# Cached pages laid over 64 partitions with two keys in each, nine projection slots to a sample, and the next stage's weights loaded ahead

## The chip, the cores and the metric

One Trainium2 chip, one core. The metric is the device time of one launch in microseconds, on the slowest (here the only) core. Smaller is better.

## The reference, cut to what matters

The kernel computes one step of a two-layer decoder for a prompt of 2048 tokens and for 8 sampled sequences of one new token each. The change lies in the second layer. Its input projection gives 21 groups of 128 channels over 2056 columns (2048 prompt tokens, 8 samples) and, in a stage of its own, the values. For each of the 8 samples, stick-breaking attention runs over 4096 cached keys, which lie in 32 pages of 128 keys in an order that a page table gives:

```python
proj = jnp.einsum('btd,dn->btn', x, w_in)
k_past = cache_k[i][page_table].reshape(bs, n_pages * PAGE_SIZE, H_C, HD_C)
z = jnp.einsum('bqhd,bkhd->bhqk', qblk, kf) + bf
log_1mb = jnp.where(causal, jax.nn.log_sigmoid(-z), 0.0)
suffix = lax.cumsum(log_1mb, axis=3, reverse=True)
excl = jnp.concatenate([suffix[..., 1:], jnp.zeros_like(suffix[..., :1])], axis=-1)
att = jnp.where(causal, jnp.exp(jax.nn.log_sigmoid(z) + excl), 0.0)
out = jnp.einsum('bhqk,bkhd->bqhd', att, vf)
```

So a key's weight needs the sum of a softplus over all later keys of its sample. A key or value row of all heads is 512 floats, 2 KB; a page is 256 KB; a sample's keys and values are 16.8 MB, those of all eight 134 MB.

## The kernel before, in words

The program is a row of stages with a barrier between them. The change touches three: `project_odd` (tiles named `po_`, line 2448), `project_values` (`pv_`, line 2998) and the start of the prompt's attention (`sp_`).

**Projection in slots.** `Channels` (line 1242) multiplies x, split into a high and a low fp32r part, with weights split the same way, three matmuls for a product (`product`, lines 119 to 121). A slot is one channel group over one block of 412 columns: 8 slices of 128 rows by 3 matmuls, 24 in all. There are 105 slots in the order of `ODD_GROUPS` (line 2441). The first five run slice by slice while x comes in (`first`); each later one writes one of five PSUM banks, which ACT copies out (`evict`, line 1371) and stores (line 1303). One raw weight buffer `po_w` holds 512 KB; its split parts are doubled. At the start DVE makes the high part of each of the 8 slices of x (`split_x`), and the low parts are made by DVE (five slices) and POOL (three, `low_x`). POOL also splits all weights but the first, and ACT issues their loads.

**Sampled attention beside it.** Pages come in through `load_pages` (line 2493): for each page a register is loaded from the table, then one DMA copies 128 rows of 2 KB to the 128 partitions. Keys go through the SP queue into 3 buffers of a pair of pages, values through the ACT queue into 3 buffers of a group of 4 pages. DVE multiplies a pair of key pages by the query (line 2648) and reduces it (line 2651); after 16 pairs it adds the bias (line 2657). ACT (exponent, logarithm, exponent: lines 2612, 2616, 2621), DVE (clamp, maximum, arguments: lines 2662 to 2675) and PE (`later`, lines 2556 and 2557: sums over later keys inside a page by a triangular matrix, and of whole pages by ones) make the weights, and PE multiplies them with the values (line 2549), 8 groups of 4 pages to a sample. A key buffer is loaded again once DVE has used it, a value buffer once PE has.

What stands where in each engine's program comes from two numbers: sample b's scores are placed at slots `START + PER*b` and after, its chain at `START + PER*(b+1)`, and its value groups from four slots later on, 8 groups over `PER` slots:

```python
START, PER = 16, 10
for g in range(NS * GROUPS):
    groups.setdefault(START + PER + 4 + g * PER // GROUPS, []).append(g)
TAIL = START + PER * (NS + 1) + 6
```

The queries come from the last block of groups 0 to 3; they are transposed at slot `Q_AT`, go out to memory and come back broadcast before DVE can begin. Each engine runs its list in order, so a wait of PE for a value buffer holds up the slots behind it.

**Value projection.** `project_values` starts behind the barrier: x tile 0, eight weight slices of 512 KB, x tile 1. ACT makes the high parts of the weights, POOL and DVE the low parts of every second slice. PE's first tile goes slice by slice behind them.

Of the kernel before, what the change touches and what calls it, by code (L numbers as in the profile page):

```python
# [17 lines left out]
F32R = mybir.dt.float32r  # L18
ALU = mybir.AluOpType
# [29 lines left out]
AT_GC = AT_SP - 36096  # L49
AT_OO = AT_GC - 3 * 4 * KT * D  # L50
# [1191 lines left out]
class Channels:  # L1242
# [7 lines left out]
    def __init__(self, s, xT, w, out, groups, banks, pinned=False):  # L1250
# [8 lines left out]
        self.x_in = [s.sem(f"x_in{k}") for k in range(KT)]  # L1259
        self.x_high = [s.sem(f"x_high{k}") for k in range(KT)]  # L1260
# [32 lines left out]

    def load_x(self, sp, slices=range(KT)):
        for k in slices:
            if k >= 4:
                sp.wait_ge(self.x_ready[k - 4], 1)
            sp.dma_start(self.stage[k % 4], self.xT[:, k, :]).then_inc(self.x_in[k], 16)
# [21 lines left out]
    def split_x(self, dve, k):  # L1320
        dve.wait_ge(self.x_in[k], 16)
        high_part(dve, self.xh[:, k, :], self.stage[k % 4]).then_inc(self.x_high[k], 1)
        if k % 3 != 1:
            dve.wait_ge(self.x_high[k], 1)
            low_part(dve, self.xl[:, k, :], self.stage[k % 4], self.xh[:, k, :]).then_inc(self.x_ready[k], 1)

    def high_x(self, act, k):
        act.wait_ge(self.x_in[k], 16)
        act.copy(self.xh[:, k, :].bitcast(F32R), self.stage[k % 4]).then_inc(self.x_high[k], 1)

    def low_x_part(self, dve, k):
        dve.wait_ge(self.x_high[k], 1)
        low_part(dve, self.xl[:, k, :], self.stage[k % 4], self.xh[:, k, :]).then_inc(self.x_ready[k], 1)

    def low_x(self, pool):
        for k in range(1, KT, 3):
            pool.wait_ge(self.x_high[k], 1)
            low_part(pool, self.xl[:, k, :], self.stage[k % 4], self.xh[:, k, :]).then_inc(self.x_ready[k], 1)
# [6 lines left out]
    def first(self, pe):  # L1345
        pe.wait_ge(self.w_low, 1)
        for k in range(KT):
            pe.wait_ge(self.x_ready[k], 1)
            for t in range(self.banks):
                mm = self.part(pe, t, k)  # L1350
                if k == KT - 1:
                    mm.then_inc(self.done, 1)
# [689 lines left out]
def rwkv_chunks(nc, ops, wc, const, y, s_out, space, tail):  # L2042
# [7 lines left out]
    with Stage(nc, "rc") as s_:  # L2050
# [372 lines left out]
        def _(pool):  # L2423
# [10 lines left out]
            for t in range(STEPS):  # L2434
# [6 lines left out]
ODD_GROUPS = ([(0, range(NBLK)), (1, range(NBLK)), (2, [NBLK - 1]), (3, [NBLK - 1, *range(NBLK - 1)]),  # L2441
               (2, range(NBLK - 1))] + [(n, range(NBLK)) for n in range(4, 21)])
# [5 lines left out]
def project_odd(nc, xT, w, z, cache_k, cache_v, table, bias, const, q_rows, cat):  # L2448
# [6 lines left out]
    HR = HC * PAGES  # L2455
    with Stage(nc, "po") as s:
# [6 lines left out]
        zs = [s.sb(f"scores{q}", [P, HC, PAGES]) for q in (0, 1)]  # L2463
        e, sp_, att, mask = (s.sb(n, [P, HC, PAGES]) for n in ("e", "softplus", "att", "mask"))
        om = s.sb("om", [P, CW])
        bt, own, idt = s.sb("bias", [P, HC]), s.sb("own", [P, HC]), s.sb("id", [P, P])
        tri, one = s.sb("tri", [P, P]), s.sb("ones", [P, P])
# [11 lines left out]
        flat = lambda t: t[:, :, :].rearrange("p h r -> p (h r)")  # L2479
        START, PER = 16, 10  # L2480
        PAGES_AT = 3
# [8 lines left out]
        TAIL = START + PER * (NS + 1) + 6  # L2490
        at = lambda table, t: table.get(t, ())

        def load_pages(eng, pages, cache, b, r, sem):
            for j in range(pages.shape[1]):
                page = eng.value_load(pt[0:1, b * PAGES + PAGES - 1 - r - j:b * PAGES + PAGES - r - j], min_val=0,
                                      max_val=cache.shape[0] - 1)
                eng.dma_start(pages[:, j, :], cache[ds(page, 1)].rearrange("o k c -> k (o c)")).then_inc(sem, 16)

        @block.sync
        def _(sp):  # L2500
# [3 lines left out]
            for dst, src in ((idt[:, :], const["ident"]), (tri[:, :], const["tri"]), (own[:, :], const["own32"]),  # L2504
                             (bt[:, :], bias.broadcast_to([P, HC]))):
                sp.dma_start(dst, src).then_inc(cst, 16)
            sp.wait_ge(tab, 16)
            for k in range(KT):
                sp.wait_ge(pj.x_ready[k], 1)
# [1186 lines left out]
```

## Time and profile before

| | |
|---|---|
| median of 3 runs | 3168.12 us (3167.9 to 3170.14) |
| the profiled execution's own time | 3175.06 us |
| its span | 3173.3 us |
| busy in the span: PE | 2920.1 us, 92% |
| DVE / ACT / POOL | 2096.5 / 1276.4 / 763.2 us |
| mean rate of the DMA engines over the span | 158 GB/s |
| `project_odd` | 1504 to 2129 us |
| `project_values` | 2129 to 2355 us |

Times in the rows are microseconds from the span's start. A busy PE is not a PE at its peak, since matmuls are pipelined: one of 128 by 412 is shown with 0.35 us, while they start 0.19 us apart. The DMA share is the mean busy share of the core's 16 DMA engines; it may stand a little over 1 in a short window.

### The profile page before, as it was taken

What the parts mean: (1) busy time and instruction counts of PE and PEld (TensorE: products, weight loads), DVE (VectorE), ACT (ScalarE), POOL (GpSimd) and SP (SyncE); (2) the same over time, 40 slices, a digit from 0 to 9 for tenths busy, and PEclk for the clock granted to TensorE, in tenths of its full rate; (3) what the DMA queues carried; (4) which work ended last, traced back from release to release, by engine and by line L of the source; (5) the groups of instructions that cost most, each with busy time, mean ns of one, the idle gap of its engine ahead of it and who ended that gap; (6) DMA issues with size and microseconds to landing.
All of it is one profiled execution on the core that took longest, in us unless ns stands there. A gap on an engine that the chain in (4) does not pass through costs nothing. (4 is left out here: it accounts for less than half of the span.)

```text
span 3173.3 us, 70051 instructions
## 1 busy us (share of the span) xinstructions
PE 2920.1 (92%) x27683; PEld 2371.2 (75%) x27683; DVE 2096.5 (66%) x3274; ACT 1276.4 (40%) x2284; POOL 763.2 (24%) x711
## 2 busy tenths in 40 slices
PE   8999999978998988998899999969989999998898
PEld 7899999966776766776798887857756666667676
DVE  9526666647676647885377777614639888886576
ACT  1325555434344335352011111111228888875332
POOL 5000000012232211110311111103127666664111
PEclk9999999989999989999999999989989999999999
DMA  6624445464444556563679999865450101008342
GB/s 212 206 96 150 153 150 150 141 167 114 100 116 92 124 154 191 158 173 92 228 219 322 354 338 336 309 197 171 140 188 3 68 22 47 15 25 249 127 157 77
DMA packets 470046, 502.30 MB, mean 158 GB/s; under 512 B 200033, under 2 KB 362834, under 8 KB 464570
## 3 DMA queue, kind: packets, MB, share of 16 engines
q1 hardware_dynamic: 373034, 338.78, 35.3%
q10 hardware_dynamic: 88176, 143.03, 13.0%
q0 software_dynamic: 8512, 16.02, 1.7%
q8 instruction: 221, 3.62, 0.5%
q14 instruction: 103, 0.84, 0.1%
HBM read 356.61 MB, written 141.31 MB: 157 GB/s over the span
## 5 line engine op out<-in xcount | busy, mean ns | idle before, releaser
L2978 POOL TENSOR_TENSOR sp_att<-sp_beta,sp_left 128x512 f32<-128x512 f32 (+3 forms) x320 | 302.3, 954 | 185.9 <-DVE sp_left L2939 171.4
L119 PE MATMUL po_acc<-po_x_high,po_w_low 128*128 128x412 f32 (+1 forms) x840 | 303.8, 362 | 20.3 <-DVE po_x_low L112 14.4
L119 PE MATMUL pe_acc<-pe_x_high,pe_w_low 128*128 128x412 f32 (+1 forms) x840 | 302.5, 360 | 3.4 <-PEq L85 3.4
L120 PE MATMUL po_acc<-po_x_low,po_w_high 128*128 128x412 f32 (+1 forms) x840 | 296.6, 353 | 0.0
L121 PE MATMUL po_acc<-po_x_high,po_w_high 128*128 128x412 f32 (+1 forms) x840 | 296.6, 353 | 0.0
L120 PE MATMUL pe_acc<-pe_x_low,pe_w_high 128*128 128x412 f32 (+1 forms) x840 | 293.5, 349 | 0.0
L121 PE MATMUL pe_acc<-pe_x_high,pe_w_high 128*128 128x412 f32 (+1 forms) x840 | 293.2, 349 | 0.0
L2939 DVE TENSOR_TENSOR_SCAN sp_left<-sp_z,sp_left,sp_zero 128x512 f32<-128x512 f32 x192 | 235.7, 1269 | 18.3 <-ACT sp_z L2900 14.0
L2648 DVE TENSOR_TENSOR po_work<-po_work,po_q 128x1024 f32<-128x1024 f32 x128 | 176.2, 1377 | 66.5 <-DMA po_work<-in_cache_k 60.7
L2892 ACT ACTIVATE sp_beta<-sp_z,sp_bias 128x512 f32<-128x512 f32 (+3 forms) x320 | 183.3, 629 | 91.5 <-PE sp_z L2827 45.9
L2430 POOL TENSOR_TENSOR rc_kt<-rc_kt,rc_mask 128x512 f32<-128x512 f32 x32 | 41.2, 1286 | 718.8 <-ACT rc_kt L2320 718.6
L119 PEld LDWEIGHTS po_acc<-po_x_high,po_w_low 128*128 128x128 f32 x840 | 160.5, 191 | 68.8 <-ACT po_o L1371 31.5
L1371 ACT COPY po_o<-po_acc 128x412 f32<-128x412 f32 (+1 forms) x105 | 52.5, 500 | 387.6 <-PE po_acc L121 355.4
L2316 ACT COPY rc_lv<-rc_bk 128x1024 f32<-128x1024 f32 (+1 forms) x192 | 129.8, 693 | 181.6 <-DVE rc_f L2406 55.2
L2841 PEld LDWEIGHTS sp_t<-sp_id,sp_att 128*128 128x128 f32 x1088 | 117.4, 141 | 97.5 <-issue 88.7
L2900 ACT ACTIVATE sp_z<-sp_z,sp_bias_neg 128x512 f32<-128x512 f32 (+3 forms) x320 | 179.2, 611 | 0.0
L2827 PE MATMUL sp_z<-sp_k,sp_q 64*128 64x512 f32 (+3 forms) x640 | 164.4, 590 | 6.4 <-PEq L85 3.2
L119 PEld LDWEIGHTS pe_acc<-pe_x_high,pe_w_low 128*128 128x128 f32 x840 | 158.3, 188 | 15.7 <-issue 14.6
L2841 PE MATMUL sp_t<-sp_id,sp_att 128*128 128x128 f32 x1088 | 152.0, 279 | 17.6 <-ACT sp_aT L2906 16.8
L120 PEld LDWEIGHTS po_acc<-po_x_low,po_w_high 128*128 128x128 f32 x840 | 160.6, 191 | 0.8
L121 PEld LDWEIGHTS po_acc<-po_x_high,po_w_high 128*128 128x128 f32 x840 | 160.3, 191 | 0.5
L2858 PE MATMUL sp_ob<-sp_aT,sp_v 128*64 128x128 f32 x2176 | 154.4, 280 | 5.9 <-DVE sp_g L2953 5.9
(493 smaller groups left out, 7027.1 us busy)
## 6 DMA issues: line engine op xcount, KB each, us to landing
po_work<-in_cache_k SPq DMA_DIRECT2D x256, 256.0 KB, 4.8
po_work<-in_cache_v ACTq DMA_DIRECT2D x256, 256.0 KB, 4.6
scratch_ops<-pe_work SPq DMA_DIRECT2D x160, 128.0 KB, 2.0
out_z<-pe_o SPq DMA_DIRECT2D x84, 206.0 KB, 2.8
out_z<-po_o ACTq DMA_DIRECT2D x84, 206.0 KB, 4.5
pe_w<-in_w_e SPq DMA_DIRECT2D x21, 512.0 KB, 5.9
po_w<-in_w_o ACTq DMA_DIRECT2D x21, 512.0 KB, 5.8
rc_opx<-scratch_ops SPq DMA_DIRECT2D x64, 160.0 KB, 3.7
```

What stands on the lines that cost most here:

```text
L119: pe.matmul(out, ll, rh, start=start, stop=False)
L120: pe.matmul(out, lh, rl, start=False, stop=False)
L121: return pe.matmul(out, lh, rh, start=False, stop=stop)
L2316: evict = lambda to, k, n: act.copy(lv[q][:, to:to + n].rearrange("p k x y c -> p x k (y c)"), b[:, :, 2 * k * CH:2 * (k + n) * CH].rearra ...
L2648: dve.tensor_tensor(kp[:, p % KR], kp[:, p % KR], qb[:, b % 2:b % 2 + 1, :].broadcast_to([P, 2, CW]), ALU.mult).then_inc(prod, 1)
L2827: mm[h] = pe.matmul(zb[h][b][:, 0:w], qt[q][r, cq], kt[q][r, ck], start=True, stop=not diagonal(n))
L2841: mm = pe.transpose(tb[h][:, b * P:(b + 1) * P], att[h][:, n % 3, b * P:(b + 1) * P], idt[:, :])
L2858: mm = pe.matmul(ob[tile(n) % 2][c, 0:P], vt[m % 2][:, 4 * g + b, c], aT[h][:, n % 2, b * P:(b + 1) * P], start=(diagonal(n) and b == 0), ...
L2892: act.activation(be[h][:, n % 4, 0:w], zb[h][n % 2][:, 0:w], ACT.Sigmoid, scale=DC ** -0.5, bias=bt[:, head:head + 1]).then_inc(sig[h], 1)
L2900: act.activation(zb[h][n % 2][:, 0:w], zb[h][n % 2][:, 0:w], ACT.Sigmoid, scale=-DC ** -0.5, bias=nbt[:, head:head + 1]).then_inc(kept[h], 1)
L2939: dve.tensor_tensor_scan(row[:, at:at + w][:, ::-1], zb[h][n % 2][:, 0:w][:, ::-1], zero.broadcast_to([P, w]), start, ALU.mult, ALU.add).t ...
L2978: pool.tensor_tensor(att[h][:, n % 3, 0:w], be[h][:, n % 4, 0:w], left[h][tile(n) % 2][:, at + 1:at + 1 + w], ALU.mult).then_inc(at_ok[h], 1)
```

## The change

1. **Pages.** Each page now goes to 64 partitions, two neighbouring keys (4 KB, one run in memory) to a partition; the pages alternate between partitions 0 to 63 and 64 to 127. Two pages fill the same buffer as before. Scores, exponents and weights are laid out by parity of the key, head and pair of pages.
2. **Sums over later keys** take three pairs of 128-column matmuls (`tri`+`tri`, `past`+`tri`, `ones`+`ones`) in place of two 256-column ones; the scan over pages is 128 wide.
3. **Slots.** `PER` is 9, `START` 12, the order of groups brings the last blocks of groups 0 to 3 forward, `Q_AT` is slot 9 in place of 13, and the first value loads stand at slots 7, 9 and 11.
4. **Start of the stage.** ACT makes the high parts of x, DVE all low parts, slice 0 in two pieces; DVE also splits the weights of the first five group entries, and SP issues the loads of entries 2 and 3. One weight load more (22 in place of 21 behind the first).
5. **Values ahead.** Once PE has finished the last slot, SP issues x tiles 0 and 1 and the first four weight slices of `project_values`, ahead of the barrier; DVE makes all eight low parts of the weights there and the first low part of x.
6. The first loads of the prompt's attention are spread over later tiles.

```diff
-ODD_GROUPS = ([(0, range(NBLK)), (1, range(NBLK)), (2, [NBLK - 1]), (3, [NBLK - 1, *range(NBLK - 1)]),
-               (2, range(NBLK - 1))] + [(n, range(NBLK)) for n in range(4, 21)])
+ODD_GROUPS = ([(0, range(NBLK)), (1, [NBLK - 1]), (2, [NBLK - 1]), (3, [NBLK - 1, *range(NBLK - 1)]),
+               (2, range(NBLK - 1)), (1, range(NBLK - 1))] + [(n, range(NBLK)) for n in range(4, 21)])
...
-        START, PER = 16, 10
-        PAGES_AT = 3
+        START, PER, BY_DVE = 12, 9, 5
+        PAGES_AT = (7, 9, 11)
...
         def load_pages(eng, pages, cache, b, r, sem):
-            for j in range(pages.shape[1]):
+            for n in range(pages.shape[1]):
...
-                eng.dma_start(pages[:, j, :], cache[ds(page, 1)].rearrange("o k c -> k (o c)")).then_inc(sem, 16)
+                at = n // 2 * 2
+                eng.dma_start(pages[half[n % 2], at:at + 2, :],
+                              cache[ds(page, 1)].rearrange("o (k j) c -> (o k) j c", j=2)).then_inc(sem, 16)
...
-                pe.matmul(stat[:, 0:HR], tri[:, :], flat(sp_), start=True, stop=True)
-                pe.matmul(stat[:, HR:2 * HR], one[:, :], flat(sp_), start=True, stop=True).then_inc(tri_pe, 1)
+                for n, (first, second) in enumerate(((tri, tri), (past, tri), (one, one))):
+                    pe.matmul(stat[:, n * HM:(n + 1) * HM], first[:, :], odd(0), start=True, stop=False)
+                    mm = pe.matmul(stat[:, n * HM:(n + 1) * HM], second[:, :], odd(1), start=False, stop=True)
+                mm.then_inc(tri_pe, 1)
...
+            sp.wait_ge(pj.done, pj.slots)
+            values_ahead.load(sp)
...
         def _(act):
+            pj.load_w(act, 1)
+            for k in range(KT):
+                pj.high_x(act, k)
...
             for k in range(KT):
-                pj.split_x(dve, k)
+                pj.low_x_part(dve, k)
+            for i in range(1, BY_DVE):
+                pj.split_w(dve, i)
...
+    def load(self, sp):
+        self.tile(sp, 0)
+        for k in range(self.FRONT):
+            self.weights(sp, k)
+        self.tile(sp, 1)
...
-            split(0)
-            for k in range(1, KT, 2):
-                dve.wait_ge(w_high, k + 1)
-                low_part(dve, wl[:, k], wr[:, k], wh[:, k]).then_inc(w_low[1], 1)
+            ahead.split_x(dve)
+            for k in range(KT):
+                ahead.low_w(dve, k)
```

How rows move. On the SP queue, where the key pages are loaded (before):

```order
L2495 TENSOR_LOAD po_pt
L2495 ISA x2
L2497 ISA
L2497 DMA po_work<-in_cache_k 128x512
L2495 TENSOR_LOAD po_pt
```

and in the changed kernel:

```order
L2499 TENSOR_LOAD po_pt
L2499 ISA x2
L2502 ISA
L2502 DMA po_work<-in_cache_k 64x1024
L2499 TENSOR_LOAD po_pt
```

The count of instructions is the same; the DMA writes 64 partitions with 1024 floats each. On PE, at the end of the projection (before):

```order
L121 MATMUL po_acc<-po_x_high,po_w_high 128x408
L2549 MATMUL po_sums<-po_work,po_att 8x512 x16
L2562 MATMUL po_outp<-po_ones,po_om 128x1 x4
L83 UNCONDITIONAL_BRANCH
L3099 UNCONDITIONAL_BRANCH
L119 MATMUL pv_acc<-pv_w_high,pv_x_low 128x512
```

and in the changed kernel:

```order
L120 MATMUL po_acc<-po_x_high,po_w_low 128x408
L121 MATMUL po_acc<-po_x_low,po_w_high 128x408
L122 MATMUL po_acc<-po_x_high,po_w_high 128x408
L84 UNCONDITIONAL_BRANCH
L3155 UNCONDITIONAL_BRANCH
L120 MATMUL pv_acc<-pv_w_high,pv_x_low 128x512
```

The last four value groups (16 matmuls) and the last sample's heads stood behind the last slot; now the last value group stands nine slots before the end, and nothing of the attention is behind slot 104.

## Rows read from the trace of the kernel before

**Rows 1.** Windows: us, busy of each engine, PEclk, DMA share, GB/s
```profile
1600.00:1650.00 50.00, 50.00 (x269) 49.88 (x268) 44.76 (x35) 5.95 (x12) 10.51 (x6) 1.00 0.83 252
...
1800.00:1850.00 50.00, 47.58 (x269) 39.08 (x267) 36.37 (x34) 5.66 (x14) 7.83 (x4) 1.00 0.99 351
...
2109.00:2130.00 21.00, 7.76 (x41) 2.30 (x40) 0.88 (x2) 2.01 (x3) 0.00 (x0) 0.60 0.47 133
```

**Rows 2.** DMA view of 1700 to 2050 us: packets, then issues with us to landing
```profile
DMA packets 65271, 119.29 MB, mean 341 GB/s; under 512 B 7249, under 2 KB 14845, under 8 KB 65235
po_work<-in_cache_k SPq DMA_DIRECT2D x185, 256.0 KB, 4.9
```

**Rows 3.** Waits, 1500 to 2130 us: who, for whom, us in total, times, longest
```profile
DVE po_work L2648 <- DMA po_work<-in_cache_k: 60.7, 55, 3.3
```

**Rows 4.** Timeline of ACT: start, duration; two samples' first exponents
```profile
1770.04 0.42 ACT L2612 ACTIVATE po_e<-po_scores 128x256 f32<-128x256 f32 x1 [5.12 <-issue]
...
1828.62 0.42 ACT L2612 ACTIVATE po_e<-po_scores 128x256 f32<-128x256 f32 x1 [4.78 <-issue]
```

**Rows 5.** Timeline of PE around a value group
```profile
1801.41 0.35 PE L121 MATMUL po_acc<-po_x_high,po_w_high 128*128 128x412 f32 x1
1801.69 1.06 PE L2549 MATMUL po_sums<-po_work,po_att 128*8 128x512 f32 x8
1802.68 0.45 PE L119 MATMUL po_acc<-po_x_high,po_w_low 128*128 128x412 f32 x1
```

**Rows 6.** Timelines of ACT, SP and PE where the two stages meet
```profile
2109.14 0.50 ACT L1371 COPY po_o<-po_acc 128x408 f32<-128x408 f32 x1 [5.16 <-PE po_acc L121]
...
2129.26 0.57 SPq L3040 DMA_DIRECT2D pv_x<-scratch_x1T  x1
...
2152.32 0.39 PE L121 MATMUL pv_acc<-pv_w_high,pv_x_high 128*128 128x512 f32 x1
```

**Rows 7.** Groups of 2130 to 2153 us: count | busy, mean ns | idle before
```profile
L112 DVE TENSOR_TENSOR pv_w_low<-pv_w,pv_w_high 128x1024 fp32r<-128x1024 f32 x4 | 12.9, 3288 | 2.9 <-ACT pv_w_high L3142 2.9
L3142 ACT CAST pv_w_high<-pv_w 128x1024 fp32r<-128x1024 f32 x8 | 8.4, 1046 | 17.0 <-DMA pv_w<-in_w_v 17.0
```

**Rows 8.** Timelines of DVE, POOL and PE at the start of the stage
```profile
1508.06 1.23 DVE L112 TENSOR_TENSOR po_w_low<-po_w,po_w_high 128x1024 fp32r<-128x1024 f32 x1
...
1523.97 2.30 DVE L112 TENSOR_TENSOR po_x_low<-po_work,po_x_high 128x2056 fp32r<-128x2056 f32 x1
...
1528.59 6.51 DVE L112 TENSOR_TENSOR po_x_low<-po_work,po_x_high 128x2056 fp32r<-128x2056 f32 x1
...
1547.91 0.45 PE L119 MATMUL po_acc<-po_x_high,po_w_low 128*128 128x412 f32 x1 [0.37 <-POOL po_w_low L112]
```

**Rows 9.** DVE: first score product, and all bias additions (ns min/median/max, first and last start)
```profile
1595.88 1.22 DVE L2648 TENSOR_TENSOR po_work<-po_work,po_q 128x1024 f32<-128x1024 f32 x1 [5.43 <-DMA po_q<-scratch_q_rows]
...
L2657 DVE TENSOR_TENSOR po_scores<-po_scores,po_bias x8: 424/426/1256, 1642.5 to 2048.7; 128x256 f32<-128x256 f32 x8
```

**Rows 10.** Timeline of the SP queue in an earlier stage: loads of 64 partitions
```profile
1216.07 0.54 SPq L416 DMA_DIRECT2D oe_w<-in_state_rwkv  x1
...
1217.96 0.60 SPq L416 DMA_DIRECT2D oe_w<-in_state_rwkv  x1
```

**Rows 11.** Windows as in rows 1, where 8 KB or 512 B packets prevail
```profile
1221.00:1223.00 2.00, 2.00 (x11) 1.67 (x10) 1.96 (x3) 1.99 (x3) 0.00 (x0) 1.00 0.95 187
...
2361.00:2363.00 2.00, 2.00 (x7) 0.66 (x4) 1.52 (x2) 2.00 (x4) 0.49 (x1) 0.50 1.03 430
...
2378.00:2379.00 1.00, 0.84 (x8) 0.70 (x7) 1.00 (x2) 1.00 (x4) 0.27 (x1) 1.00 0.98 167
2500.50:2501.50 1.00, 0.72 (x7) 0.48 (x5) 1.00 (x2) 1.00 (x4) 0.87 (x1) 1.00 1.16 340
```

**Rows 12.** DMA view of 2136 to 2141 us: 4 KB packets to 128 partitions
```profile
DMA packets 569, 2.07 MB, mean 414 GB/s; under 512 B 64, under 2 KB 64, under 8 KB 569
q1 hardware_dynamic: 569, 2.07, 102.6%
```

More of the change, by code:

```diff
@@ L1296, in load_x @@
             if k >= 4:
[L1297 to L1298 removed]
+                sp.wait_ge(self.x_ready[k - 4], len(self.pieces(k - 4)))
+            for sem, c in self.pieces(k):
+                sp.dma_start(self.stage[k % 4][:, c], self.xT[:, k, c]).then_inc(sem, 16)
     def store(self, eng, t):
@@ L1347, in first @@
         for k in range(KT):
+            last = len(self.pieces(k))
             pe.wait_ge(self.x_ready[k], 1)
             for t in range(self.banks):
+                if t == 2 and last == 2:
+                    pe.wait_ge(self.x_ready[k], 2)
                 mm = self.part(pe, t, k)
@@ L2462, in project_odd @@
         qb = s.sb("q", [P, 2, CW])
-        zs = [s.sb(f"scores{q}", [P, HC, PAGES]) for q in (0, 1)]
-        e, sp_, att, mask = (s.sb(n, [P, HC, PAGES]) for n in ("e", "softplus", "att", "mask"))
+        zs = [s.sb(f"scores{q}", [P, 2, HC, PAIRS]) for q in (0, 1)]
+        e, sp_, att = (s.sb(n, [P, 2, HC, PAIRS]) for n in ("e", "softplus", "att"))
+        mask, before = s.sb("mask", [P, HC, PAIRS]), s.sb("before", [P, HC, PAIRS])
         om = s.sb("om", [P, CW])
         bt, own, idt = s.sb("bias", [P, HC]), s.sb("own", [P, HC]), s.sb("id", [P, P])
-        tri, one = s.sb("tri", [P, P]), s.sb("ones", [P, P])
+        tri, past, one = s.sb("tri", [P, P]), s.sb("past", [P, P]), s.sb("ones", [P, P])
         pt = s.sb("pt", [1, NS * PAGES], I32)
@@ L2534, in _ @@
         def _(pool):
-            pj.low_x(pool)
-            for i in range(1, len(ODD_GROUPS)):
+            for i in range(BY_DVE, len(ODD_GROUPS)):
                 pj.split_w(pool, i)
@@ L2600, in _ @@
                     pj.store(act, t)
-                    if t in pj.opens and i + 2 < len(ODD_GROUPS):
+                    if t in pj.opens and 4 <= i + 2 < len(ODD_GROUPS):
                         pj.load_w(act, i + 2)
-                if t == PAGES_AT:
-                    for g in range(VR):
-                        values(g)
+                if t in PAGES_AT:
+                    values(PAGES_AT.index(t))
                 for g in at(groups, t - 1):
@@ L3037, in tile @@
             def tile(t):
-                if t >= 2:
-                    sp.wait_ge(x_low, t - 1)
-                sp.dma_start(xr[:, t % 2, :, 0:rows(t)], x[:, :, t * P:t * P + rows(t)]).then_inc(x_in[t % 2], 16)
+                sp.wait_ge(x_low, t - 1)
+                ahead.tile(sp, t)
             def keys(b):
@@ L3050, in store @@
                     sp.dma_start(ops[:, i, j, at:at + w], t[q][:, 0:w]).then_inc(g_st[q], 16)
-            tile(0)
-            for k in range(KT):
-                sp.dma_start(wr[:, k, :], w[:, k, :]).then_inc(w_in[k], 16)
-            tile(1)
+            for k in range(ahead.FRONT, KT):
+                ahead.weights(sp, k)
             for dst, src in ((wt[:, :], alpha_w), (bt[:, :], alpha_b), (mask[:, :], const["reset"][:, 0:GW]),
@@ L3071, in _ @@
                     scores.load_keys(sp)
-                    for h in (0, 1):
-                        sp.wait_ge(o_st[h], 32)
-                    scores.load_values(sp)
+                if t == FIRST + NU + 1:
+                    scores.load_queries(sp)
+            scores.load_gates(sp)
+            for h in (0, 1):
+                sp.wait_ge(o_st[h], 32)
+            scores.load_values(sp)
             for j in (0, 1):
@@ L3091, in tile @@
                 low_part(pool, flat(xl, h), flat(xr, h), flat(xh, h)).then_inc(x_low, 1)
-            tile(0)
-            for k in range(0, KT, 2):
-                pool.wait_ge(w_high, k + 1)
-                low_part(pool, wl[:, k], wr[:, k], wh[:, k]).then_inc(w_low[0], 1)
             for t in range(1, TT + 1):
@@ L3602, in constants @@
     reset[:, SEQ:] = 0
+    pages, later = h[:, None] == h[None, :], h[:, None] < h[None, :]
     jm = np.zeros((P, P))
@@ L3607, in constants @@
             "levels": np.stack([level(m) for m in (1, 2, 4, 8, 16, 32)], 1), "reset": reset,
-            "neg": np.where(i[None, :] < i[:, None], 0, -1e30), "tri": i[:, None] >= i[None, :],
+            "neg": np.where(i[None, :] < i[:, None], 0, -1e30), "tri": later | (pages & (i[:, None] >= i[None, :])),
+            "past": later | (pages & (i[:, None] > i[None, :])),
             "own32": np.tile(np.eye(32)[:, 0:HC], (4, 1)), "jm": jm,
```

130 lines of the change are left out of this document (81 added, 49 removed).

## The prediction, made before the changed kernel was run

> **What bounds the kernel now.** I read the windows of the stage first, then its waits, then the timelines where it begins and ends. While the eight samples run, two things are nearly full at once: the DMA engines are busy with a share of 0.99 and move 351 GB/s, and PE is busy for 47.6 of 50 us, DVE for 36.4 [rows 1]. In the waits DVE stands for key pages 55 times, 60.7 us in all, but never longer than 3.3 us [rows 3]. Two neighbouring samples' first exponents lie 58.6 us apart [rows 4]: that is the pace of ten slots. Where PE ran without a break, 269 matmuls took 50.0 us [rows 1], 0.186 us each, so a slot's 24 are 4.48 us; a value group puts 1.27 us in place of one such step and costs 1.08 us [rows 5]. Ten slots with eight groups are 44.8 + 8.6 = 53.4 us, and chain, heads and short waits make the rest. The page traffic is as tight: 5488 us of engine time (0.98 x 16 x 350) went into 58,022 data packets, 94.6 ns for one of about 2 KB [rows 2]; a sample's 8192 packets are 48.4 us of the 16 engines, and its ten slots' stores and weights some 8 us more. So PE and DMA run neck and neck, and whatever slows the pages slows the slots.
>
> Behind the last slot PE runs the last sample's groups with waits, and the next stage begins with loads behind the barrier: from the last eviction at 2109.1 to the end of the first value tile at 2152.7 are 43.6 us [rows 6], PE clock 0.60 in most of it [rows 1].
>
> **The change part by part.** The sum is made against the profiled execution (span 3173.3, own time 3175.06 us, 6.9 above the median); differences are then taken off the median, 3168.1.
>
> *Start of the stage.* A low part of x takes DVE 2.30 us alone and 6.51 us beside one of POOL; slot 5 starts at 1547.9 [rows 8]. With POOL out of it, DVE makes eight at 2.3 us (18.4), ACT the high parts; the loads of 8.4 MB at the best rate shown, about 420 GB/s [rows 11, 12], are 20 us. I put slot 5 at 1537.5, less 10.4 us. Slots 5 and 6 then are the only ones of their weights, and a 512 KB load with its split (DVE: 0.7 + 1.23 us [rows 8]) is just longer than 4.48 us: 2 us back. Net **-8.5 us**.
>
> *Slots and attention on PE.* The last four groups move ahead of the end of the slots: 4 x 1.08 = 4.3 us. Six matmuls of 128 columns for two of 256 are 768 columns for 512; at most 0.5 us a sample by the 1.06 us that a group's matmuls with 512-column outputs take [rows 5]: 4 us. The 58.6 us of a sample become 58.6 - 4.5 = 54.1 where nothing else binds. These only move work: the sum of slots and groups is the same. **+8 us**, so with the start the last slot ends where it did, near 2109.
>
> *Where the stages meet.* After the last slot SP issues at once what now waits for the barrier at 2129.3. The tiles and eight weight slices, 5.2 MB, were paced by DMA (ACT waited 17.0 us for weights) and then by low parts at 3.3 us each on two engines [rows 7]; alone on DVE one takes 1.23 us [rows 8]. From the last slot: 0.5 us to the first load, 5.2 MB at 414 GB/s [rows 12] with some 2 us of latency 15 us, last high and low part 2.3 us, six matmuls 1.5 us: 19.5 for 43.6, **-24 us**. The cover of its middle part is the DMA time itself; if the barrier came later than 8 us (the front load's 3.1 MB), the gap would grow.
>
> *The pages.* This decides. No row of before shows a page on 64 partitions. From below, a 4 KB packet to 128 partitions took (1.026 x 16 x 5 us) / 505 = 162 ns [rows 12], so two keys cost 162 ns where two packets of 94.6 cost 189: a sample would need 42 us in place of 48, and the DMA has room for nine slots. From above, the trace has loads to 64 partitions. Two of 512 KB with 8 KB rows were issued at 1216.07 and 1217.96, to the lower and then the upper half [rows 10]. While the second ran, the engines were busy with a share of 0.95 and moved 187 GB/s; loads of 8 KB rows to all 128 partitions moved 430 GB/s at 1.03 [rows 11]. Per busy share this is 197 against 417, a factor 2.1. It isn't the number of engines, since they were all busy; the packets took twice as long. A second place agrees: 512-byte rows to 64 partitions gave 167 GB/s at 0.98, to 128 partitions 340 at 1.16, a factor 1.7 [rows 11]. 
> The Trainium skill (SBUF — State Buffer, "Door 1: The DMA port swizzle") says the same in its own terms: partitions 0 to 63 reach only 8 of 16 ports. Its section "Can I just issue two DMAs to hit both halves?" measured only 6% more for two concurrent DMAs on the two halves than for one; by that the packet would take 1.9 times as long and the kernel about 3310 us, and no row here shows two queues on the two halves.
>
> Now keys come on SP's queue and values on ACT's, each alternating halves. When both queues stand in the same half, the factor is 2; when in different ones, an engine pair meets for part of a packet, between 1 (never) and 2 (in step), 1.5 in the middle. Half of the time each: (2 + 1.5) / 2 = **1.75**, my value; 2.0 and 1.5 are its bounds, 1.0 the bound of the other case. If the whole packet stretches, it takes 162 x 1.75 = 284 ns; if a fixed part stays as it is (2 x 94.6 - 162 = 27 ns by the two packet sizes), 27 + 135 x 1.75 = 263. I take 270 ns, which is 16 x 4096 / 270 = 242 GB/s. In the same way 2.0 gives 309 ns and 212 GB/s, 1.5 gives 234 ns and 280 GB/s.
>
> Length of the stream: the first scores hang on the queries' slot. They stood at 1595.9 [rows 9]; four slots (18 us) and the start (10 less 2) earlier they stand at 1570. Sample 0's keys took 46.6 us to 1642.5 [rows 9], now about 50, to 1619; its weights are ready and the value groups begin near 1640. From there 121 MB of the 134 are still to come. 121 MB at 242 GB/s are 500 us, and stores and weights of 70 slots at 0.82 us 57 more: the last group is done near 2197. Nine slots stand behind it, 40 us: the last slot ends at **2237, +128 us** over 2109. PE is then idle a third of the time, and its queue's order makes the slots wait with the groups.
>
> Sum: +128 - 24 = +104 us; 3168.1 + 104 = **3272 us**. The loads of the prompt's attention that move (part 6) are hidden under tiles of 12 us either way: nothing.
>
> **The rivals.**
>
> *A. The halves cost nothing and the larger row helps.* Two queues in different halves fill both, or the slow loads of rows 11 were slow by their place in memory (8 KB out of every 16 KB). For it: page reads are one run in memory, and 4 KB rows save up to 14%. Against it: 512-byte loads at another place were slow too. Then the slots end near 2109 and the rest gains 24 us: 3144 us, between 3128 (the waits of the samples shrink too, by 16) and 3156. The point from which it decides: the stream must end 104 us earlier than in my sum, 121 MB in 396 us, 306 GB/s, a packet of 214 ns or a factor of 1.35. Below that the change is faster.
>
> *B. In step.* All 16 engines start each DMA together, so that pairs stay in step even in different halves: factor 2.0 throughout, 571 us + 57, last slot at 2308, +199 - 24: 3343 us.
>
> *C. Well mixed.* 1.5 throughout: 432 + 57, last slot at 2169, +60 - 24: 3204 us.
>
> *D. The pages are as fast as in A, but DVE becomes the bound.* Its 36.4 of 50 us [rows 1] are 43 us a sample, of 54 now, and it waits for ACT in order. If a sample still took 58.6 us, the attention would end 8 x 4.5 = 36 us later than planned, just inside the 40 us of the nine slots behind it: 3144 to 3150, a part of A's range.
>
> **How the numbers follow.** My case with B and C has 0.78 (forecast 0.44, B 0.17, C 0.17), A with D 0.22, of which 0.19 faster and 0.03 within the 0.2% (6 us) that a measurement of this kernel can tell. Range of the likeliest side: 3204 to 3343. Those of A must be reached, or more than 2 in 10 would be left out: 3130 to 3343. Faster 0.19, same 0.03, slower 0.78.
>
> **What would show it.** Right: from 1650 to 2150 us the DMA share is near 1 at 210 to 290 GB/s, page loads land after 6 to 9 us in place of 4.9, samples' first exponents lie 68 to 88 us apart, PE waits for value pages by more than 100 us, and the last slot ends 60 to 200 us later; at the same time slot 5 starts near 1537, and from the last slot to the first value tile's end are about 20 us. Wrong: samples 54 us apart with the DMA at 340 GB/s or more (A), or DVE without idle time (D).

## The result, and the profile after

| | before | changed |
|---|---|---|
| median | 3169.13 us (3167.9 to 3170.59, 4 runs) | 3294.72 us (3289.72 to 3297.15, 4 runs) |
| ratio | | 1.0391, 95% interval 1.0368 to 1.0413 |
| the profiled execution's own time, its span | 3175.06, 3173.3 us | 3297.15, 3295.3 us |
| `project_odd`: last slot's eviction | 2109.1 us | 2249.1 us |
| first value tile's copy begins | 2152.7 us | 2279.7 us |

The changed kernel is 3.9% slower, 125.6 us; the forecast was 3272 (+104). Between the two profiled executions, 127.0 us more stand at the first value tile, and the rest of the program gives back 5.0.

Windows of the changed kernel, columns as in [rows 1]:

```profile
1620.00:1650.00 30.00, 10.26 (x50) 9.86 (x49) 25.39 (x24) 1.61 (x4) 0.00 (x0) 0.67 0.82 212
...
1800.00:1850.00 50.00, 39.11 (x200) 31.36 (x192) 28.05 (x25) 3.56 (x9) 4.29 (x3) 0.86 1.03 277
...
2200.00:2250.00 50.00, 48.96 (x269) 46.26 (x268) 0.69 (x1) 5.55 (x12) 3.44 (x2) 1.00 0.19 62
```

In the window 1800 to 1850 that stood in [rows 1] the DMA engines are as full as before, 1.03, but move 277 GB/s in place of 351. PE took 200 steps for 269. At 2200 to 2250 nine slots run behind the pages, while the DMA has nothing to do.

The DMA view of 1700 to 2050 us, as in [rows 2]:

```profile
DMA packets 32008, 93.68 MB, mean 268 GB/s; under 512 B 5689, under 2 KB 11116, under 8 KB 31979
q10 hardware_dynamic: 19359, 52.85, 58.5%
q1 hardware_dynamic: 12620, 40.51, 44.6%
po_work<-in_cache_k SPq DMA_DIRECT2D x151, 256.0 KB, 8.8
po_work<-in_cache_v ACTq DMA_DIRECT2D x149, 256.0 KB, 11.6
```

Half as many packets moved a fifth less. In the records of single packets, the 20,352 of 4096 bytes took 254.7 ns in the mean (median 260). A few of them, some 1,100, are the projection's weights, which go to all partitions. A page of keys lands 8.8 us after its issue (before 4.9), a page of values 11.6 us.

Waits of 1500 to 2260 us, to be held against [rows 3]:

```profile
DVE po_work L2662 <- DMA po_work<-in_cache_k: 200.9, 102, 5.5
...
PE po_sums L2558 <- DMA po_work<-in_cache_v: 82.5, 30, 7.9
...
PE po_stat L2566 <- DVE po_softplus L2682: 24.6, 3, 19.7
```

DVE's wait for keys went from 60.7 to 200.9 us. PE waits 82.5 us for value pages, and once 19.7 us for the first sample's softplus: that is the hole at 1620 to 1650 above.

ACT's timeline, two samples' first exponents, as in [rows 4]; with all eight, 1628.97 to 2142.9, samples lie 73.4 us apart, before 59.6 (1648.9 to 2066.4):

```profile
1773.74 0.42 ACT L2624 ACTIVATE po_e<-po_scores 128x256 f32<-128x256 f32 x1 [5.20 <-issue]
1848.19 0.42 ACT L2624 ACTIVATE po_e<-po_scores 128x256 f32<-128x256 f32 x1 [5.16 <-issue]
```

Timelines of ACT, SP and DVE where the stages meet, as in [rows 6]:

```profile
2249.05 0.50 ACT L1371 COPY po_o<-po_acc 128x408 f32<-128x408 f32 x1 [3.97 <-PE po_acc L122]
2262.39 3.89 ACT L3198 CAST pv_w_high<-pv_w 128x1024 fp32r<-128x1024 f32 x4 [10.89 <-PEq L86]
```

```profile
2249.68 2.41 SPq L2749 DMA_DIRECT2D pv_w<-in_w_v  x4
2252.13 0.57 SPq L2746 DMA_DIRECT2D pv_x<-scratch_x1T  x1
2252.74 2.82 SPq L2540 DMA_DIRECT2D scratch_cat<-po_oc  x1
2262.38 1.77 SPq L2749 DMA_DIRECT2D pv_w<-in_w_v  x4
```

```profile
2264.28 9.17 DVE L113 TENSOR_TENSOR pv_w_low<-pv_w,pv_w_high 128x1024 fp32r<-128x1024 f32 x8
2273.45 0.27 DVE L3303 MEMSET pv_vec<- 128x256 f32 x1
2273.76 0.69 DVE L108 CAST pv_x_high<-pv_x 128x1024 fp32r<-128x1024 f32 x1
2279.73 1.22 DVE L3299 COPY pv_o<-pv_acc 128x1024 f32<-128x1024 f32 x1 [5.28 <-PE pv_acc L122]
```

The front loads go out at once, but the next stage begins 13.3 us after the last slot. The small store of the sampled attention (`scratch_cat`), which the barrier waits for, was issued behind 3.1 MB on the same queue. By the packet records its 512 packets of 32 bytes ran at 2259.6 to 2260.5, behind all of these loads, and it was complete at 2261.1; the next stage began 1.3 us later. That interval is 1.3 us in the kernel before too (2128.0 to 2129.3). The store's input was ready only at 2251.8, although the last value matmul stood at 2207: ACT makes the gates for it behind its last slot. ACT and DVE stand idle for it by 10.9 and 10.6 us, though the first weights are there. From the last slot to the first value tile's end are 30.7 us, before 43.6.

### The profile page after: what moved, and what is told of

It is laid out like the page before. It is cut to its first block and busy times, and to the rows that moved or that the text cites. A ratio compares the mean times of both kernels' runs of the same rounds, so it can differ in the third digit from the quotient of the medians.

```text
span 3295.3 us, 70189 instructions
## 1 busy us (share of the span) xinstructions
PE 2955.4 (90%) x27747; PEld 2396.4 (73%) x27747; DVE 2085.4 (63%) x3283; ACT 1292.1 (39%) x2293; POOL 722.8 (22%) x697
## 5 line engine op out<-in xcount | busy, mean ns | idle before, releaser
L120 PE MATMUL po_acc<-po_x_high,po_w_low 128*128 128x412 f32 (+1 forms) x840 | 315.0, 375 | 15.5 <-DVE po_x_low L113 13.5
L121 PE MATMUL po_acc<-po_x_low,po_w_high 128*128 128x412 f32 (+1 forms) x840 | 305.7, 364 | 0.0
L122 PE MATMUL po_acc<-po_x_high,po_w_high 128*128 128x412 f32 (+1 forms) x840 | 304.7, 363 | 0.0
L2662 DVE TENSOR_TENSOR po_work<-po_work,po_q 128x1024 f32<-128x1024 f32 x128 | 169.2, 1322 | 209.8 <-DMA po_work<-in_cache_k 200.9
L120 PEld LDWEIGHTS po_acc<-po_x_high,po_w_low 128*128 128x128 f32 x840 | 168.6, 201 | 77.4 <-issue 57.8
L121 PEld LDWEIGHTS po_acc<-po_x_low,po_w_high 128*128 128x128 f32 x840 | 168.3, 200 | 1.2
L122 PEld LDWEIGHTS po_acc<-po_x_high,po_w_high 128*128 128x128 f32 x840 | 166.9, 199 | 1.0
L108 POOL CAST po_w_high<-po_w 128x1024 fp32r<-128x1024 f32 x18 | 21.1, 1171 | 664.8 <-PE po_acc L122 664.8
```

The lines of the kernel that those rows point to most:

```text
L120: pe.matmul(out, ll, rh, start=start, stop=False)
L121: pe.matmul(out, lh, rl, start=False, stop=False)
L122: return pe.matmul(out, lh, rh, start=False, stop=stop)
L2662: dve.tensor_tensor(kp[:, p % KR], kp[:, p % KR], qb[:, b % 2:b % 2 + 1, :].broadcast_to([P, 2, CW]), ALU.mult).then_inc(prod, 1)
```

## The experiments

Time is the median; "against before" is the difference to the median of the kernel before, measured beside it on the same chip, with the 95% interval of the ratio in brackets. The kernel before itself ranged from 3160.6 to 3180.9 us, so differences of less than some 4 us can't be told apart.

| run | us | against before |
|---|---|---|
| half_pages_alone | 3279.6 | +107 (1.0299 to 1.0367) |
| ten_slots | 3262.8 | +90 (1.0261 to 1.0329) |
| half_2k_rows | 3306.2 | +135 (1.0392 to 1.0437) |
| interleaved_9 | 3206.8 | +34 (1.0064 to 1.0136) |
| interleaved_10 | 3195.3 | +25 (1.0075 to 1.0109) |
| old_layout_9 | 3176.1 | +3 (0.9997 to 1.0032) |
| old_layout_10 | 3165.0 | -5 (0.9977 to 1.0001) |
| no_ahead_10 | 3166.2 | -4 (0.9973 to 0.9999) |
| act_store_10 | 3167.0 | -3 (0.9980 to 1.0002) |
| weights_later | 3158.1 | -10 (0.9961 to 0.9985) |
| start_14 | 3153.7 | -17 (0.9936 to 0.9964) |
| start_13 | 3146.9 | -24 (0.9911 to 0.9938) |

### half_pages_alone: only the pages' place, in the old kernel

```diff
+                at = j // 2 * 2
...
-                eng.dma_start(pages[:, j, :], cache[ds(page, 1)].rearrange("o k c -> k (o c)")).then_inc(sem, 16)
+                eng.dma_start(pages[j % 2 * 64:j % 2 * 64 + 64, at:at + 2, :],
+                              cache[ds(page, 1)].rearrange("o (k j) c -> (o k) j c", j=2)).then_inc(sem, 16)
```

> The kernel before, with one edit: each page goes to 64 partitions, two keys of 4 KB to a partition, alternating halves, by the same queues. All else is the old code, so the sampled attention sums over later keys in a wrong order (its part of the output is another). Theory 1 (loads into one half of the partitions share a path; packets of the changed kernel took about 253 ns): the samples go from 58.6 us apart to about 74, eight of them give +122 us, and there are no slots behind the attention to wait: 3290 us (3270 to 3310), DMA share near 1 at 265 to 280 GB/s. Theory 2 (the slowness comes from nine slots a sample, DVE or the start of the stage, not from the pages): within 15 us of 3169.

Measured: 3279.6 us, +107. The DMA view of 1700 to 2050:

```profile
DMA packets 32971, 95.47 MB, mean 273 GB/s; under 512 B 5821, under 2 KB 11805, under 8 KB 32942
q10 hardware_dynamic: 20079, 54.03, 58.1%
q1 hardware_dynamic: 12863, 41.10, 44.9%
```

Samples stand 73.7 us apart (1652.6 to 2168.5), packets take 249.8 ns. So the pages alone, without nine slots, new sums or a new start, make 107 of the 126 us; theory 2 falls.

### old_layout_9: all of the change but its pages and sums

```diff
-                at = n // 2 * 2
-                eng.dma_start(pages[half[n % 2], at:at + 2, :],
-                              cache[ds(page, 1)].rearrange("o (k j) c -> (o k) j c", j=2)).then_inc(sem, 16)
+                eng.dma_start(pages[:, n, :], cache[ds(page, 1)].rearrange("o k c -> k (o c)")).then_inc(sem, 16)
...
-                for n, (first, second) in enumerate(((tri, tri), (past, tri), (one, one))):
...
+                pe.matmul(stat[:, 0:HR], tri[:, :], flat(sp_), start=True, stop=True)
+                pe.matmul(stat[:, HR:2 * HR], one[:, :], flat(sp_), start=True, stop=True).then_inc(tri_pe, 1)
```

> The changed kernel with its parts 3 to 6 (nine slots, start, values ahead), but pages, scores and sums over later keys as before: 128 partitions by 2 KB. Theory 1 (the halves alone cost the time): DMA at about 350 GB/s, packets of 95 ns, samples about 56 us apart (48.4 us of pages and 7.2 of stores and weights), the last slot near 2105 to 2112, then 30 us to the first value tile as in the changed kernel: 3150 to 3162 us. Theory 2 (nine slots or the start are at fault): over 3250 us.

Measured: 3176.1 us, no gain. Packets of 2 KB are back at 94.4 ns, so the layout of the pages, with its sums, cost 122 us (125.6 less 3.1). But I had expected 3150 to 3162. Its windows, and the evictions of its slots (duration in ns, first and last start):

```profile
1700.00:1750.00 50.00, 45.16 (x258) 35.62 (x256) 37.99 (x33) 5.04 (x11) 8.75 (x4) 1.00 0.98 348
...
2100.00:2125.00 25.00, 25.00 (x139) 24.95 (x138) 0.00 (x0) 2.51 (x5) 0.00 (x0) 1.00 0.14 51
```

```profile
L1371 ACT COPY po_o<-po_acc x105: 481/502/508, 1531.4 to 2136.0; 128x412 f32<-128x412 f32 x84, 128x408 f32<-128x408 f32 x21
```

Samples stand 58.8 us apart with nine slots, against 59.6 with ten before: the old pages nearly fill the DMA too (0.98 in the window above, 0.95 from 1650 to 2050), and nine slots mostly leave work for the end, 42 us of slots from the last value matmul at 2093.9 to 2136.

### interleaved_9: even and odd partitions in place of halves

```diff
-                eng.dma_start(pages[half[n % 2], at:at + 2, :],
+                eng.dma_start(pages[n % 2:P:2, at:at + 2, :],
...
-    pages, later = h[:, None] == h[None, :], h[:, None] < h[None, :]
+    pages, later = i[:, None] % 2 == i[None, :] % 2, i[:, None] % 2 < i[None, :] % 2
```

> The changed kernel with one edit: the two pages of a pair go to the even and to the odd partitions in place of the lower and the upper half (the two constant matrices follow). Row size (4 KB), number of partitions per transfer (64), queues, bytes and all other work stay. Theory 1 (the half is what is slow: all engines write into one half's path): a transfer now reaches both halves, packets fall from 253 to about 165 ns, DMA is no longer full, samples are about 54 to 57 us apart: 3140 to 3162 us. Theory 3 (64 partitions a transfer, or 4 KB rows, or the memory side is slow, wherever they land): unchanged, 3285 to 3305 us.

Measured: 3206.8 us, 92 less than the changed kernel against their own runs of before, but not the 3140 to 3162 I expected. The same windows and DMA view:

```profile
1800.00:1850.00 50.00, 45.08 (x247) 35.88 (x245) 35.50 (x33) 4.78 (x13) 6.89 (x4) 0.93 0.89 305
```

```profile
DMA packets 37840, 110.64 MB, mean 316 GB/s; under 512 B 6737, under 2 KB 13265, under 8 KB 37804
q10 hardware_dynamic: 23291, 63.51, 51.0%
q1 hardware_dynamic: 14513, 46.72, 39.4%
```

The share fell from 1.03 to 0.91 while the rate rose: a 4 KB packet takes 186.4 ns (median 159), with the same row, as many partitions (64) and the same queues. So which partitions a transfer reaches is the cause, and it makes 92 of the layout's 122 us. Two packets of 2 KB are 2 x 94.4 = 189 ns, so larger rows saved nothing in the mean; by the medians (159 for 2 x 84 = 168 ns) they saved 5%. What makes this kernel 31 us slower than old_layout_9, with the DMA less full, isn't settled: an issue takes 475 ns on SP (338 with 128 partitions), there are six matmuls for two, and PE's waits and the clock (0.93 above) are both worse.

### half_2k_rows: one half, but rows of 2 KB

```diff
-                              cache[ds(page, 1)].rearrange("o (k j) c -> (o k) j c", j=2)).then_inc(sem, 16)
+                              cache[ds(page, 1)].rearrange("o (j k) c -> (o k) j c", j=2)).then_inc(sem, 16)
```

> The changed kernel with one edit: a page still goes to 64 partitions of one half, but a partition takes keys k and k + 64 in place of two neighbours, so each is a row of 2 KB (the sums over later keys then run in another order of keys). It fills the fourth field beside 2 KB rows to all partitions (packets of 94 ns), 4 KB rows to every second partition (186 ns) and 4 KB rows to one half (254 ns). Theory 1 (the half is slow, whatever the row): 2 KB packets take 130 to 150 ns, the DMA share stays at 1.03 with 250 to 275 GB/s, and the kernel takes 3285 to 3320 us. Theory 3 (rows of 4 KB are slow in a half, as where packets are long): packets of 95 to 105 ns and 3170 to 3215 us.

Measured: 3306.2 us, and in its DMA view:

```profile
DMA packets 50253, 91.93 MB, mean 263 GB/s; under 512 B 5584, under 2 KB 10831, under 8 KB 50225
q10 hardware_dynamic: 28351, 51.79, 59.6%
q1 hardware_dynamic: 21874, 39.82, 46.2%
```

Packets of 2 KB took 134.4 ns. The four fields, mean and median in ns:

| | 2 KB row | 4 KB row |
|---|---|---|
| both halves reached | 94.4 / 84 (old_layout_9) | 186.4 / 159 (interleaved_9) |
| one half | 134.4 / 138 | 254.7 / 260 (the changed kernel) |

The half costs a factor 1.42 and 1.37 by the means, 1.64 and 1.64 by the medians, whatever the row. Theory 3 falls. Mean and median differ because the means of the upper row hold a few very long packets (one in twenty over 361 ns, even with 4 KB rows to every second partition), while in the lower row most packets are longer: with 4 KB rows, nine in ten took 164 to 319 ns.

### ten_slots: the changed kernel with PER 10

```diff
-        START, PER, BY_DVE = 12, 9, 5
+        START, PER, BY_DVE = 12, 10, 5
```

> The changed kernel with ten slots to a sample in place of nine. In the changed kernel the last value matmul stands at 2207 and the last slot's eviction at 2249: nine slots run behind the pages with an idle DMA. Theory 1 (the stream of pages sets the time, slots fill its gaps): they now run inside it, the stream is only some 7 us longer by their stores and weights, the last slot ends near 2216 to 2222, so 30 us less: 3260 to 3272 us. Rival (PE, not DMA, paces the samples): each sample one slot of 4.5 us longer, the end stays: 3290 to 3300 us.

Measured: 3262.8 us, 36 less than the changed kernel, each against its own before. The last value matmul stands at 2217.2, the last eviction at 2216.9: the slots ran inside the stream, which got 10 us longer. This is the term of nine slots behind the pages, 40 us in the prediction.

### old_layout_10 and interleaved_10: ten slots with the other layouts

The same one-line edit on old_layout_9 and interleaved_9.

> The kernel of old_layout_9 (the change's parts 3 to 6 with the old pages and sums) with ten slots to a sample in place of nine. In old_layout_9 the samples stayed 58.8 us apart at a DMA share of 0.98 and 42 us of slots ran behind them. Theory 1 (the page stream also sets the pace of the old layout; nine slots only leave work behind it): the stream gets 7 us longer by the stores and weights of nine more slots, the last slot ends at 2100 to 2108 in place of 2136: 3140 to 3152 us, faster than both kernels. Rival (PE with its waits paces the samples): each sample 4.5 us longer, no gain: 3170 to 3180 us.

> The kernel of interleaved_9 (4 KB rows on every second partition) with ten slots. Theory 1: as with the old layout some 30 us less than with nine: 3172 to 3182 us. If 4 KB rows with both halves reached had any gain over 2 KB rows it would be under old_layout_10; I expect it 15 to 30 us over that, since its samples stood 61.7 us apart with nine slots, not 58.8.

Measured: 3165.0 and 3195.3 us, each only 8 less than with nine slots, against 30 expected, and the intervals with nine and ten slots overlap. The last slot of old_layout_10 stands at 2124.6: 11 us earlier than in old_layout_9, but its samples now lie 62.1 us apart, with the DMA at 0.94 from 1650 to 2050. That is 3.3 us more than with nine slots, most of the 4.5 us of a slot, so the pace is rather the rival's (PE with its waits) than the stream's. What slowed PE is what the last runs look for. Interleaved rows stay 30 us above the old layout.

### no_ahead_10 and act_store_10: the meeting of the stages

```diff
-            values_ahead.load(sp)
...
+            ahead.load(sp)
             for k in range(ahead.FRONT, KT):
                 ahead.weights(sp, k)
```

> The kernel of old_layout_10, but x tiles 0 and 1 and the first four weight slices of the value projection are issued behind the barrier again (DVE still makes all low parts there). By the prediction's term (-24 us for the stage meeting, most of it from the loads ahead) it is over 15 us slower than old_layout_10. By the trace of the changed kernel the loads ahead hold up the store that the barrier waits for, so they save little: between 2 us faster and 10 us slower than old_layout_10.

```diff
-            sp.wait_ge(out, 1)
-            sp.dma_start(cat[0:4, :, SEQ:COLS].rearrange("n p c -> p n c"), oc[:, :, :]).then_inc(stored, 16)
-            sp.wait_ge(stored, 16)
...
+            act.wait_ge(out, 1)
+            act.dma_start(cat[0:4, :, SEQ:COLS].rearrange("n p c -> p n c"), oc[:, :, :]).then_inc(stored, 16)
+            act.wait_ge(stored, 16)
```

> The kernel of old_layout_10, but the last store of the sampled attention (16 KB), which the barrier waits for, goes out on ACT's queue in place of SP's, where it stood behind 3.1 MB of loads ahead. In the changed kernel it was issued 3.7 us after the last slot and the barrier came 13.3 us after it. Theory (the store's place in the queue delays the barrier): the barrier comes 6 to 9 us after the last slot, the last four weight slices start earlier: 3 to 8 us faster than old_layout_10. Rival (the DMA engines are full anyway, the store is late on any queue, or the weights set the end): the same within 2 us.

Measured: 3166.2 and 3167.0 us beside 3165.0 for old_layout_10: neither edit can be seen in the time. SP's timeline of no_ahead_10, then of old_layout_10:

```profile
2127.39 0.39 SPq L2533 DMA_DIRECT2D scratch_cat<-po_oc  x1
2130.44 0.56 SPq L2735 DMA_DIRECT2D pv_x<-scratch_x1T  x1
```

```profile
2128.27 2.87 SPq L2534 DMA_DIRECT2D scratch_cat<-po_oc  x1
2137.93 1.76 SPq L2739 DMA_DIRECT2D pv_w<-in_w_v  x4
```

Without loads ahead the next stage begins 6.1 us after the last slot (2124.3), with them 13.3 us after it (2124.6). The first value tile is copied 28.4 and 30.5 us after the last slot. So the loads ahead gain nothing: they hold up the barrier by what they save. On ACT's queue the store did little better: the stage began 11.8 us behind the last slot and the tile 27.9, since the full DMA engines delay it there too: the store landed 7.5 us after its issue, where without loads ahead it took 1.8 (no_ahead_10). So its theory (a barrier after 6 to 9 us, 3 to 8 us gained) falls and the rival holds.

### start_13, start_14, weights_later: where a sample's chain falls

```diff
-        START, PER, BY_DVE = 12, 10, 5
+        START, PER, BY_DVE = 13, 10, 5
```

> The kernel of act_store_10 with the samples placed one slot later (START 13). In the trace of old_layout_10 PE stands 5.3 us for sample 0's softplus, since its scores, begun at once, are paced by the key pages and not by slots. Theory: that wait goes, and the last slot ends some 4 us earlier; the last value groups move one slot later and take back about 1 us: 0 to 5 us less than act_store_10, 3160 to 3166 us. Rival (the stream of pages from the first key to the last is what lasts until 2125): no change or up to 4 us slower.

> The same with START 14. The last value groups now stand one slot behind the last projection slot, and more of the last sample's groups fall into the stage's end: if the wait for sample 0 was all there was to gain, 1 to 6 us over start_13. Rival (PE's waits in the samples fall further as keys run ahead of their slots): 2 to 6 us under start_13.

```diff
-                    if t in pj.opens and 4 <= i + 2 < len(ODD_GROUPS):
-                        pj.load_w(act, i + 2)
+                    if t - 1 in pj.opens and 4 <= pj.slot[t - 1][0] + 2 < len(ODD_GROUPS):
+                        pj.load_w(act, pj.slot[t - 1][0] + 2)
```

> The kernel of act_store_10 (START 12) with each weight load issued by ACT one slot later. With START 12 and ten slots the third ACT step of every sample's chain (the exponent that makes the weights) stands in the slot in which ACT also issues a 512 KB weight load; with START 13 it stands one slot behind it. ACT came to that step 5.6 us after the work before it in act_store_10 and 4.9 us in start_13, and PE's waits for it were 14.8 and 9.8 us. Theory (this collision in ACT's order, and the lower clock that PE's waits bring, is what START 13 removed): 3145 to 3155 us as with START 13, PE's waits for the weights near 10 us. Rival (the gain of START 13 lies in something else, such as when the first sample begins or where groups fall at the end): as act_store_10, 3160 to 3170 us.

Measured: 3146.9, 3153.7 and 3158.1 us, beside 3167.0 for act_store_10. START 13 gained 21 us against their own runs of before, where 0 to 5 were expected; START 14 gave 7 of them back, where 1 to 6 were expected if the wait for sample 0 was all, and its rival (2 to 6 us under start_13) falls. PE's waits, 1550 to 2120 us, and the window 1650 to 2050, of act_store_10, of start_13 and of weights_later:

```profile
PE po_stat L2556 <- DVE po_softplus L2673: 16.9, 8, 7.0
PE po_sums L2549 <- ACT po_att L2622: 14.8, 7, 2.9
...
1650.00:2050.00 400.00, 377.20 (x2020) 313.41 (x2019) 288.98 (x247) 38.34 (x86) 49.71 (x26) 0.95 0.93 320
```

```profile
PE po_stat L2556 <- DVE po_softplus L2673: 10.6, 8, 4.5
PE po_sums L2549 <- ACT po_att L2622: 9.8, 7, 1.7
...
1650.00:2050.00 400.00, 385.19 (x2138) 320.08 (x2137) 286.21 (x258) 40.78 (x91) 54.88 (x26) 0.99 0.95 331
```

```profile
PE po_stat L2556 <- DVE po_softplus L2673: 17.2, 8, 7.4
PE po_sums L2549 <- ACT po_att L2622: 10.6, 7, 2.0
...
1650.00:2050.00 400.00, 382.41 (x2111) 317.46 (x2110) 292.97 (x250) 39.73 (x89) 48.66 (x26) 0.98 0.95 328
```

ACT's timeline of old_layout_10 shows the collision: the weight load and four page loads are issued ahead of the exponent for which PE waits.

```profile
1766.71 0.45 ACTq L1294 DMA_DIRECT2D po_w<-in_w_o  x1
1768.12 3.50 ACTq L2497 DMA_DIRECT2D po_work<-in_cache_v  x4
1771.73 0.42 ACT L2625 ACTIVATE po_att<-po_scores 128x256 f32<-128x256 f32 x1 [5.44 <-issue]
```

Moving the weight load away, at the same START, brought PE's wait for this exponent from 14.8 to 10.6 us, as with START 13 (9.8), the granted clock from 0.95 to 0.98, and the time down by 7 of the 21 us (intervals 0.9961 to 0.9985 and 0.9980 to 1.0002, which just overlap). The wait's fall is clear: the three kernels with the same attention and START 12 (old_layout_10, no_ahead_10, act_store_10) show 14.2 to 15.6 us for it. The clock's is less so, since these three have 0.95 to 0.97. So the collision is shown in the wait, and it makes about a third of the gain as far as these runs can resolve it. The rest lies in what else START moves; PE's waits for the softplus (17.2 against 10.6) point to the samples' first half, but no run tells it apart.

start_13 beats both kernels: 0.9924 of before, with the old page layout.

## Why the prediction was right, and where it was wrong

**The pages: the cause right, the size good in part by luck.** Forecast 270 ns for a packet, measured 254.7. By the forecast's two ways the factor is 1.57 (a whole packet of 162 ns stretched) or 1.69 (27 + 135 x 1.69), between C's 1.5 and my 1.75. But 162 ns is a packet of one queue alone. In the full stream the kernel before had 4 KB packets too, those of its weights, at 170.6 ns in the mean (1700 to 2050 us), and interleaved_9 has 186.4: against these the mean grew by 1.49 and 1.37 only. A base that was too small met a factor that was too large; 1.75 on 186.4 ns would have been 326. By the medians (159 to 260, factor 1.64) both were nearly right. That a packet takes between 1 and 2 times its own time is what the records show (164 to 319 ns for nine in ten, 1.0 to 2.0 times 159).
The value stream ran from 1658.6 to 2207.0, 548 us for 557. It began 18.6 us later than forecast: sample 0's keys took 56 us in place of 50 (first score at 1572.8), and PE then stood 19.7 us for its chain. It ended 10 us later. By the forecast's own steps packets of 254.7 ns make 470 + 57 = 527 us, so the stream also lasted 21 us longer than its packets account for; this offset, too, helped the sum. Behind it lay 42 us of slots for 40: ten_slots took 36 of them away. So the last slot came at 2249, 12 us after my 2237. The loads to 64 partitions in [rows 10, 11] were the right witness for a sign, and overstated the size (2.1 and 1.7). The page of the Trainium skill that I named (SBUF — State Buffer, "Can I just issue two DMAs to hit both halves?") would have made the factor 1.9 and the time 3310; the traces show 1.4 to 1.7, however it is counted, with two queues that alternate halves. By the steps of my sum the factor 1.9 gives a packet of about 294 ns and 3315 us. That time is as near to the measured 3294.7 as my 3272, since other terms of the sum missed by as much; it is the packet that speaks for the lower factor.

Of the signs that I had named, two more did not come, beside the 20 us at the meeting of the stages (below): PE waited 82.5 us for value pages, not over 100, and value pages landed after 11.6 us, outside 6 to 9. PE was idle for a fifth of the time (busy for 450.8 of 550 us from 1650 to 2200), not for a third.

**Where the stages meet: the mechanism failed.** The term was -24, the trace shows -12.9 (30.7 for 43.6). "After the last slot SP issues at once what now waits for the barrier" was so. But the store that the barrier waits for was queued behind it, which the prediction had not looked at, though it had set the condition itself (a barrier within 8 us; it came at 13.3). So the step that failed is the cover of the 15 us of loads: the last four weight slices did not follow the front ones but started 13.3 us after the last slot. What is left isn't the loads ahead either: no_ahead_10, without them, has 28.4 us. Before, 13.0 of the 43.6 us were the last sample's value groups (last slot 2109.1, last group 2122.1), and these now stand among the slots.

**The start of the stage: the cause right, the gain not kept.** Slot 5 began near 1537, as forecast. DVE's low parts took 2.30 us each. But old_layout_10, with this start and the old pages, has its last slot at 2124.6 and its last group at 2124.9, before at 2109.1 and 2122.1. The 10 us were lost again, and PE shows where: in its waits for the chain (14.9 and 14.2 us in all, before 8.6 and 9.9) and in a granted clock of 0.95 and 0.97 where before had 1.00 and 0.98.

**The slots: the term of +8 was wrong in what it left out.** I wrote that nine slots with fast pages bring samples 54 us apart. old_layout_9 shows 58.8, with a DMA share of 0.95 that leaves little room, and interleaved_9 shows that 4 KB rows don't shorten the stream (186.4 ns for 189), where I had taken 162 from a window of five microseconds with one queue. Rival A's 3144 us was therefore too low as a price for this change without slow halves: the two forms of it that ran gave 3176 (old_layout_9) and 3207 (interleaved_9).

**The sum.** +104 against 125.6 in the medians and 122.1 between the profiled executions: 12 us from the stream and its tail, 11 from the meeting of the stages. Against them stand the 5.0 us that the stages behind gave back, which I had at nothing (part 6) and didn't trace. Rivals B and C missed by their factor, D didn't come up: DVE waited 200.9 us for keys.

## What to carry to other kernels

Ask of a load not only how long its rows are but which partitions it reaches: a transfer into partitions 0 to 63 or 64 to 127 alone made the packets 1.4 times as long by the mean, and the DMA share stayed at 1.03 and showed nothing; read share and GB/s together. When loads are pulled ahead of a barrier, look for the last small store that the barrier waits for and what it now stands behind. Before slots are taken out of a software pipeline, ask what sets its pace: where it is the stream, as in the changed kernel, the slots only come back at the end, nearly in full (36 of 42 us in ten_slots); with the old pages only 8 us came back.

## What the runs showed of the hardware

- A transfer of 256 KB to 64 partitions takes the issuing engine 469 ns on SP and 485 on ACT (4 KB rows), 599 and 607 (2 KB rows), against 338 and 345 to 128 partitions (medians). There are half as many packets, or as many, but the issue is longer.
- The slowing of a half reached other traffic: stores' packets of 1648 bytes, from all partitions, took 82 ns in place of 69 in the mean (medians 72 and 69), and the weights' 4 KB packets beside the pages of half_2k_rows 236 ns, where the kernel before has 171 (medians 227 and 159).
- Small loads behind large ones: on the same queue the 16 KB store landed 8.4 us after its issue (old_layout_10), on the other queue 7.5 us (act_store_10), with no loads ahead 1.8 us (no_ahead_10).
- In these kernels the granted clock was lower where PE waited more, though no run shows that the waits alone set it: 0.88 from 1650 to 2050 us in the changed kernel, 0.95 in act_store_10 and 0.99 in start_13, where 118 more steps are recorded on PE in those 400 us than in act_store_10. At 0.186 us they are 22 us: PE's waits in the attention fell by 7 (32.6 to 25.5), and 0.04 of 400 us, 16, came from the clock. A few records of PE can be missing, so the sum is rough.
